# Conditioning dots of layer 1 dealt to two projections, and two weight blocks converted ahead of the silu of the conditioning vectors

## The chip, the cores and the metric

The kernel runs as one program on 1 core of a Trainium2 chip. Its engines are TensorE (matrix products, PE in the rows), VectorE (DVE), ScalarE (ACT), GpSimd (POOL) and SyncE (SP), which here only issues transfers. Every number is a device time in microseconds (us). The metric is the time of one execution of the whole program, as a median over several runs.

## The reference, cut to what matters

Two layers of a diffusion trunk are computed for 128 context tokens and 512 latent tokens at once, 640 columns in all, with 1024 channels. Each layer has a mixer and a PEER channel mixer, and both are modulated by vectors that depend on the conditioning alone:

```python
mod = (jax.nn.silu(cond) @ adaln_w[i] + adaln_b[i])[:, None, :]
sh1, sc1, g1, sh2, sc2, g2 = jnp.split(mod, 6, axis=-1)
hn = rmsnorm(x, norm_mix[i]) * (1 + sc1) + sh1
if i % 2 == 0:
    m = even_mixer(hn, even_w_in[j], even_conv_w[j], even_w_out[j], grid)
else:
    m, s_f, s_b = ssd_mixer(...)
x = x + g1 * m
hn = rmsnorm(x, norm_ffn[i]) * (1 + sc2) + sh2
x = x + g2 * peer(hn, peer_w_q[i], peer_keys[i], peer_u[i], peer_v[i])
```

`adaln_w[i]` is a matrix of 1024 by 6144, so that `mod` has 48 slices of 128 channels in each layer, and each slice is wanted for two conditioning vectors (`c` and `c_ctx`). Layer 1's `mod` is first used when layer 1 begins; sc1 and sh1 are the first 16 of the 48 slices.

## The kernel before, in words

The program is a row of stages, and each stage is a block that all engines enter and leave together. For layer 0 the stages around the change are: `first_adaln` (16 slices of layer 0's modulation on TensorE), a norm, the projection `even_in` (16 weight blocks), the Fourier and convolution stage, `split_into`, the projection `even_out` (8 weight blocks), a norm, the projection `q0` (16 weight blocks), and then the rest of `peer`. In layer 1 the projection `q1` has the shape of `q0`.

**`project_split` (L404)** is the helper behind all four projections. It takes one weight block of 128 by 1024 at a time from `ring`, eight slots that SyncE refills by halves of four blocks (2 MB each). ScalarE copies a block to the upper part of `wide` in fp32r (L465), GpSimd subtracts that from the block for the lower part (L472), and TensorE makes 48 products of the block (L400: 8 chunks, three products of parts, two halves of the tokens). `wide` has two slots, so that ScalarE converts block n+2 when TensorE has finished block n. VectorE takes a finished block out of PSUM: two copies in `even_in`, `q0` and `q1` (L523), three `scalar_tensor_tensor` that add to `xT` in `even_out` (L535). There are two sets of PSUM banks, so TensorE waits for the eviction of block n before it begins block n+2.

**The side work** rides in a projection where `side=(layer, lo, hi)` is given: `even_in` has 32 slices of layer 0 (two for each block), `q0` has all 48 slices of layer 1 (three for each block). A slice is computed on VectorE as two dots along the row, one for each conditioning vector: L502 multiplies a row tile of 128x1024 by a row of `crow` and sums. SyncE loads the conditioning rows `crow` (1 MB, L442), then the slices in pairs of 1 MB, of which two are in the chip at once (L438); a pair's load waits for the dots on the pair that it overwrites. ScalarE makes `crow` into its silu (L460). VectorE does the dots of a block's share, then that block's eviction, in the order of the program:

```python
for o in range(n_blocks):
    for e in range(o * per, (o + 1) * per):
        ...
    dve.wait_ge(wide_used, o + 3)
    evacuate(o, ps[o % 2]).then_inc(pair_free, 1)
```

Before, ScalarE waits for `crow` and makes its silu ahead of the first conversion:

```python
if side is not None:
    act.wait_ge(cond_in, 16)
    nc.scalar.activation(crow[:, :, :], crow[:, :, :], ACT.Silu).then_inc(cond_silu, 1)
with act.Fori(0, n_blocks // SLOTS) as i:
```

After the last block VectorE adds the bias (L509) and forms `scale_mix` or `scale_ffn` (L305).

Of the kernel before, what the change touches and what calls it, by code (L numbers as in the profile page):

```python
# [23 lines left out]
ACT = mybir.ActivationFunctionType  # L24
# [41 lines left out]
SLOTS = 8  # L66
# [73 lines left out]
def hybrid_trunk(nc, stream, keys, wdt, xin, cols_d, rows_d, masks_d, dft_d, state_in, cond_rows, ada_rows, table0, table1, y_out, state_out,  # L140
                 gates_dram, hidden_dram):
    ctx = ExitStack()
    with ctx:
# [252 lines left out]
        def split_matmuls(outs, w_hi, w_lo, moving, c, start, stop):  # L396
# [4 lines left out]
                                            start=start and n == 0, stop=stop and n == 2)  # L401
            return last

        def project_split(tag, n_blocks, moving, evacuate, chunks=NCH, side=None):  # L404


# [3 lines left out]
            with ExitStack() as ph:  # L410
# [5 lines left out]
                if side is not None:  # L416
                    layer, lo, hi = side
                    n_side = hi - lo
                    PAIRS_IN = 2
                    crow = sb(f"crow{tag}", [P, 2, D_MODEL], into=ph)  # L420
                    rows_in = sb(f"ada_in{tag}", [P, PAIRS_IN, 2, D_MODEL], into=ph)
                    junk = sb(f"ada_junk{tag}", [P, 2, D_MODEL], into=ph)
                    cond_in, cond_silu, ada_dotted, ada_biased = (
                        sem(f"{n}_{tag}") for n in ("cond_in", "cond_silu", "ada_dotted", "ada_biased"))
                    pair_in = [sem(f"ada_pair_in{j}_{tag}") for j in range(PAIRS_IN)]
                    per = n_side // n_blocks
                    begin_row = lo - N_FIRST if layer == 0 else N_ADALN - N_FIRST + lo
                with nc.Block() as block:
                    @block.sync
                    def _(sp):  # L430
                        if side is None:
                            feed(sp, first, n_blocks)
                            return

                        def load_pair(p):
                            if p >= PAIRS_IN:
                                sp.wait_ge(ada_dotted, 4 * (p - PAIRS_IN + 1))
                            sp.dma_start(rows_in[:, p % PAIRS_IN, :, :],  # L438
                                         ada_rows[begin_row + 2 * p:begin_row + 2 * p + 2].rearrange("b p n -> p b n"))\
                              .then_inc(pair_in[p % PAIRS_IN], 16)  # L440

                        sp.dma_start(crow[:, :, :], cond_rows).then_inc(cond_in, 16)  # L442
                        pairs = n_side // 2
                        ahead = min(PAIRS_IN, pairs)
                        for p in range(ahead):
                            load_pair(p)
                        for s in range(n_blocks):
                            while ahead < pairs and 2 * (ahead - PAIRS_IN + 1) <= per * (s + 1):
                                load_pair(ahead)
                                ahead += 1  # L450
                            if s % HALF_RING == HALF_RING - 1 and first + SLOTS + s < N_BLOCKS:
                                sp.wait_ge(blocks_used, first + s + 1)
                                load_half(sp, s // HALF_RING % 2, first + SLOTS + s + 1 - HALF_RING)

                    @block.scalar
                    def _(act):
                        act.sem_inc(wide_used, 2)
                        if side is not None:
                            act.wait_ge(cond_in, 16)
                            nc.scalar.activation(crow[:, :, :], crow[:, :, :], ACT.Silu).then_inc(cond_silu, 1)  # L460
                        with act.Fori(0, n_blocks // SLOTS) as i:
                            for s in range(SLOTS):
                                loaded(act, s, i + first // SLOTS)
                                act.wait_ge(wide_used, i * SLOTS + (s + 1))
                                nc.scalar.activation(wide[:, s % 2, 0, :], ring[:, s, :], ACT.Copy).then_inc(hi_done, 1)  # L465

                    @block.gpsimd
                    def _(pool):
# [21 lines left out]
                    @block.vector  # L490
                    def _(dve):
                        dve.sem_inc(pair_free, 2)
                        if side is not None:
                            dve.wait_ge(cond_silu, 1)
                            for o in range(n_blocks):
                                for e in range(o * per, (o + 1) * per):
                                    p, at_ = e // 2, rows_in[:, e // 2 % PAIRS_IN, e % 2, :]
                                    dve.wait_ge(pair_in[p % PAIRS_IN], (p // PAIRS_IN + 1) * 16)
                                    if e >= 2:
                                        dve.wait_ge(ada_dotted, 2 * (e - 1))  # L500
                                    for k, out in ((0, junk[:, e % 2, :]), (1, at_)):
                                        nc.vector.tensor_tensor_reduce(  # L502
                                            out=out, in0=at_, in1=crow[:, k, :], scale=1.0, scalar=0.0, op0=ALU.mult, op1=ALU.add,
                                            accum_out=mods_of[layer][:, lo + e, k:k + 1]).then_inc(ada_dotted, 1)
                                dve.wait_ge(wide_used, o + 3)
                                evacuate(o, ps[o % 2]).then_inc(pair_free, 1)
                            dve.wait_ge(ada_dotted, 2 * n_side)
                            to, bias = adaln_bias(layer, lo, hi)
                            nc.vector.tensor_tensor(to, to, bias, ALU.add).then_inc(ada_biased, 1)  # L509
                            dve.wait_ge(ada_biased, 1)  # L510
                            for comp in (SC1, SC2):
                                if lo <= comp * NCH < hi:
                                    adaln_scale(layer, comp)
                            return
                        with dve.Fori(0, n_blocks // SLOTS) as i:
                            for o in range(per_round):
                                dve.wait_ge(wide_used, i * SLOTS + ((o + 1) * each + 2))
                                evacuate(i * per_round + o, ps[o % 2]).then_inc(pair_free, 1)
# [72 lines left out]
        def even_mixer():  # L591
            with ExitStack() as ph:
# [90 lines left out]
                between.close()  # L683
                y2 = sb("y2_even", [P, NCH, 2, TOK], F32R, into=ph)
                split_into(y2, pT, NCH)
                project_split("even_out", N_EVEN_OUT, [(y2, part) for part in HALVES], add_gated_halves(G1, 0))

        def grid(u):

# [48 lines left out]
        def peer(layer):  # L738
# [7 lines left out]
            with ExitStack() as sparse_life:  # L746
# [5 lines left out]
                with ExitStack() as h_life:  # L752
                    h2 = sb(f"h2{tag}", [P, NCH, 2, DENSE], F32R, into=h_life)
                    idT = sb(f"idT{tag}", [P, 3, DENSE], into=h_life)
                    with ExitStack() as ph:
                        qT = sb(f"qT{tag}", [P, N_WQ, TOK], into=ph)
                        ranges = (slice(0, DENSE), slice(DENSE, TOK))
                        with ExitStack() as s_life:
# [1 line left out]
                            norm_modulate(f"f{layer}", None, scale_of(scale_ffn[layer]), shift_of(SH2, layer),  # L760
                                          split=list(zip((h2, h2s), ranges)), by_token=by_token)
                            project_split(f"q{layer}", N_WQ, [(h2, slice(0, DENSE)), (h2s, slice(0, SPARSE))],
                                          copy_halves(qT, ranges), side=(1, 0, N_ADALN) if layer == 0 else None)
                        keysT = sb(f"keysT{tag}", [P, 2 * PEER_HEADS * KEYS], into=ph)
                        top_keys(layer, tag, ph, h2, qT, keysT, idT, ids, sgate)
                    scatter_gates(layer, tag, h2, idT, by_token, ids, sgate, acc)
# [1334 lines left out]
```

## Time and profile before

| what | value |
|---|---|
| median of 3 runs | 4914.34 us (4910.57 to 4922.31) |
| the profiled execution, its own time | 4908.72 us |
| its span from the first to the last instruction | 4906.9 us |
| TensorE busy | 4500.9 us, 92% of the span |
| TensorE weight loads busy | 3709.5 us, 76% |
| VectorE busy | 3193.5 us, 65% |
| ScalarE busy | 1435.8 us, 29% |
| GpSimd busy | 981.5 us, 20% |
| mean granted TensorE clock | 0.956 |

The profiled execution has a time of its own beside the span of its instructions. The shares are averages over stages with different limits; the stages that the change touches lie in the first 531 us of the span. TensorE's granted clock is given as a share of 2.4 GHz, so that 0.50 is 1.2 GHz.

### The profile page before, as it was taken

What the parts mean: (1) busy time and instruction counts of PE and PEld (TensorE: products, weight loads), DVE (VectorE), ACT (ScalarE), POOL (GpSimd) and SP (SyncE); (2) the same over time, 40 slices, a digit from 0 to 9 for tenths busy, and PEclk for the clock granted to TensorE, in tenths of its full rate; (3) what the DMA queues carried; (4) which work ended last, traced back from release to release, by engine and by line L of the source; (5) the groups of instructions that cost most, each with busy time, mean ns of one, the idle gap of its engine ahead of it and who ended that gap; (6) DMA issues with size and microseconds to landing.
All of it is one profiled execution on the core that took longest, in us unless ns stands there. A gap on an engine that the chain in (4) does not pass through costs nothing. (4 is left out here: it accounts for less than half of the span.)

```text
span 4906.9 us, 60603 instructions
## 1 busy us (share of the span) xinstructions
PE 4500.9 (92%) x21860; PEld 3709.5 (76%) x21860; DVE 3193.5 (65%) x7358; ACT 1435.8 (29%) x2432; POOL 981.5 (20%) x564
## 2 busy tenths in 40 slices
PE   6968899999979999969899779799999997999997
PEld 5857788788868888857777665588878886888886
DVE  4829776699966666635656521226759998666665
ACT  2121233344433333322222220113323443333333
POOL 1113344322210000001211220124442222000000
PEclk8989999999989999989999889899999998999998
DMA  4414433588888888701101010123348888888882
GB/s 185 179 53 179 171 129 129 210 322 331 323 317 299 285 283 297 267 22 41 41 24 43 29 62 34 52 80 135 128 148 309 322 330 323 304 285 297 286 282 104
DMA packets 343772, 937.13 MB, mean 191 GB/s; under 512 B 14544, under 2 KB 145872, under 8 KB 305872
## 3 DMA queue, kind: packets, MB, share of 16 engines
q1 hardware_dynamic: 305360, 662.94, 38.1%
q0 software_dynamic: 38272, 272.65, 14.6%
q8 instruction: 48, 0.79, 0.1%
q14 instruction: 92, 0.75, 0.0%
HBM read 796.59 MB, written 138.94 MB: 191 GB/s over the span
## 5 line engine op out<-in xcount | busy, mean ns | idle before, releaser
L400 PE MATMUL ov_p<-acts_p,wide_v_p 128*128 128x512 f32 x6144 | 1396.8, 390 | 58.8 <-DVE acts_p L1330 58.8
L400 PEld LDWEIGHTS ov_p<-acts_p,wide_v_p 128*128 128x128 f32 x6144 | 1155.7, 188 | 299.5 <-issue 59.1
L400 PE MATMUL hl_p<-h_p,wide_late_p 128*128 128x512 f32 x3072 | 733.1, 394 | 10.9 <-DVE wide_late_p L1152 10.9
L400 PE MATMUL he_p<-h_p,wide_early_p 128*128 128x512 f32 x3072 | 727.1, 397 | 1.9 <-POOL wide_early_p L833 1.7
L400 PEld LDWEIGHTS he_p<-h_p,wide_early_p 128*128 128x128 f32 x3072 | 576.2, 188 | 146.2 <-issue 8.0
L400 PEld LDWEIGHTS hl_p<-h_p,wide_late_p 128*128 128x128 f32 x3072 | 570.0, 189 | 123.8 <-issue 11.4
L1318 DVE TENSOR_TENSOR wide_v_p<-ring,wide_v_p 128x1024 fp32r<-128x1024 f32 x256 | 313.8, 1226 | 445.1 <-ACT wide_v_p L1287 445.1
L1287 ACT ACTIVATE wide_v_p<-ring 128x1024 fp32r<-128x1024 f32 x256 | 271.3, 1060 | 908.6 <-PE ov_p L400 895.6
L833 POOL TENSOR_TENSOR wide_early_p<-ring,wide_early_p 128x1024 fp32r<-128x1024 f32 x128 | 338.5, 2645 | 463.4 <-ACT wide_early_p L889 463.4
L1030 POOL DMA_INDIRECT rows_v_p<-in_table,ids_p x128 | 123.2, 963 | 1218.2 <-DVE acc_p L1351 1172.5
L1030 POOL DMA_INDIRECT rows_late_p<-in_table,ids_p x128 | 225.0, 1758 | 705.6 <-DVE acc_p L1182 642.2
L1161 DVE TENSOR_SCALAR hot_p<-rows,idT_p 128x128 f32<-128x128 f32 x1024 | 347.5, 339 | 0.0
L400 PE MATMUL psq<-h_p,wideq 128*128 128x512 f32 x768 | 268.2, 450 | 44.7 <-POOL wideq L472 30.5
L1112 ACT ACTIVATE wide_late_p<-ring 128x1024 fp32r<-128x1024 f32 x128 | 135.3, 1058 | 546.7 <-PE hl_p L400 542.0
L1591 PE MATMUL gs<-hT,ring 128*128 128x320 f32 x1024 | 287.9, 440 | 5.4 <-ACT su L1679 2.8
L1160 DVE TENSOR_SCALAR hot_p<-rows,idT_p 128x128 f32<-128x128 f32 x1024 | 287.2, 281 | 0.0
L1591 PEld LDWEIGHTS gs<-hT,ring 128*128 128x128 f32 x1024 | 197.8, 195 | 87.4 <-issue 7.6
L1100 PEld LDWEIGHTS pg_p<-hot_p 128*128 128x128 f32 x2048 | 248.2, 191 | 10.0
L1100 PE MATMUL pg_p<-hot_p 128*128 128x128 f32 x2048 | 249.0, 275 | 0.0
L894 ACT ACTIVATE gelu_early_p<-he_p 128x512 f32<-128x512 f32 x128 | 76.6, 598 | 506.3 <-PE he_p L400 506.3
L1326 DVE TENSOR_TENSOR hidden_in_p<-hidden_in_p,gbuf_p 128x512 f32<-128x512 f32 x256 | 175.2, 684 | 54.7 <-DMA hidden_in_p<-hidden 54.7
L400 PEld LDWEIGHTS psq<-h_p,wideq 128*128 128x128 f32 x768 | 146.6, 191 | 79.6 <-POOL wideq L472 31.1
(285 smaller groups left out, 5949.5 us busy)
## 6 DMA issues: line engine op xcount, KB each, us to landing
ring<-in_stream SPq DMA_DIRECT2D x162, 2048.0 KB, 9.0
gates<-staged_p SPq DMA_DIRECT2D x32, 2048.0 KB, 10.6
gbuf_p<-gates SPq DMA_DIRECT2D x64, 1024.0 KB, 13.0
hidden_in_p<-hidden SPq DMA_DIRECT2D x64, 1024.0 KB, 15.5
hidden<-gelu_early_p SPq DMA_DIRECT2D x128, 256.0 KB, 2.0
hidden<-gelu_late_p SPq DMA_DIRECT2D x128, 256.0 KB, 3.8
ada_inq<-in_ada_rows SPq DMA_DIRECT2D x24, 1024.0 KB, 4.9
ada_ineven_in<-in_ada_rows SPq DMA_DIRECT2D x16, 1024.0 KB, 5.0
```

What stands on the lines that cost most here:

```text
L400: last = nc.tensor.matmul(out, lhsT=w, rhs=rhs[:, c, part, cols_], start=start and n == 0, stop=stop and n == 2)
L833: nc.gpsimd.tensor_tensor(wide[:, e % 2, 1, :], ring[:, e, :], wide[:, e % 2, 0, :].bitcast(F32), ALU.subtract).then_inc(blocks_used, 1)
L894: nc.scalar.activation(gelu[:, e % 2, :], hs[e % 2][:, 0:DENSE], ACT.Gelu).then_inc(gelu_done, 1)
L1030: pool.indirect_dma_start(out=rows_in[:, k % slots, :], out_offset=None, in_=(table0, table1)[layer], in_offset=bass.IndirectOffsetOnAxis( ...
L1100: last = nc.tensor.matmul(pg[j][g][:, i * P:(i + 1) * P], lhsT=hot2[:, j, g * EACH + i, :], rhs=hot1[:, j, g * EACH + i, :], start=True, s ...
L1112: nc.scalar.activation(wide[:, m % 2, 0, :], ring[:, m % SLOTS, :], ACT.Copy).then_inc(his_done, 1)
L1160: v.tensor_scalar(hot2[:, m % 2, i, :], row("iota"), idT[:, 1, token:token + 1], None, ALU.is_equal)
L1161: last = v.tensor_scalar(hot1[:, m % 2, i, :], row("iota"), idT[:, 0, token:token + 1], idT[:, 2, token:token + 1], ALU.is_equal, ALU.mult)
L1287: nc.scalar.activation(wide[:, b % 4, 0, :], ring[:, b % SLOTS, :], ACT.Copy).then_inc(whi_done, 1)
L1318: v.tensor_tensor(wide[:, b % 4, 1, :], ring[:, b % SLOTS, :], wide[:, b % 4, 0, :].bitcast(F32), ALU.subtract).then_inc(blocks_used, 1)
L1326: v.tensor_tensor(a, a, gbuf[:, j, :, e, :], ALU.mult).then_inc(mul_done, 1)
L1591: last = mm(ps[h][:, 0:HALF_TOK], lhsT=ring[:, HALF_RING * half + b, c * P:(c + 1) * P], rhs=hT[:, c, HALVES[h]], start=c == 0, stop=c == ...
```

## The change

Layer 1's 48 slices are dealt to two projections: `even_out` gets the first 16 (two for each of its 8 blocks) and `q0` the other 32 (two for each of its 16 blocks instead of three). `even_out` so gets a load of `crow`, eight loads of pairs, a silu, 32 dots, and a bias and a scale at its end. In every projection with side work ScalarE converts blocks 0 and 1 first and makes the silu behind them, ahead of block 2; its loop over blocks is written out there. The semaphores of the side work are now made once and counted on from one projection to the next (`uses`, `dots_before`, `rounds_before`).

```diff
+        PAIRS_IN = 2
+        side_sems = [sem("ada_" + n) for n in ("cond_in", "cond_silu", "dotted", "side_biased")] + \
+                    [sem(f"ada_pair_in{j}") for j in range(PAIRS_IN)]
+        side_done = [0, 0]
...
-                    cond_in, cond_silu, ada_dotted, ada_biased = (
-                        sem(f"{n}_{tag}") for n in ("cond_in", "cond_silu", "ada_dotted", "ada_biased"))
-                    pair_in = [sem(f"ada_pair_in{j}_{tag}") for j in range(PAIRS_IN)]
+                    cond_in, cond_silu, ada_dotted, ada_biased, *pair_in = side_sems
+                    uses, rows_before = side_done
+                    side_done[:] = uses + 1, rows_before + n_side
+                    dots_before, rounds_before = 2 * rows_before, rows_before // (2 * PAIRS_IN)
...
-                                sp.wait_ge(ada_dotted, 4 * (p - PAIRS_IN + 1))
+                                sp.wait_ge(ada_dotted, dots_before + 4 * (p - PAIRS_IN + 1))
...
                         act.sem_inc(wide_used, 2)
-                        if side is not None:
-                            act.wait_ge(cond_in, 16)
-                            nc.scalar.activation(crow[:, :, :], crow[:, :, :], ACT.Silu).then_inc(cond_silu, 1)
-                        with act.Fori(0, n_blocks // SLOTS) as i:
-                            for s in range(SLOTS):
-                                loaded(act, s, i + first // SLOTS)
-                                act.wait_ge(wide_used, i * SLOTS + (s + 1))
-                                nc.scalar.activation(wide[:, s % 2, 0, :], ring[:, s, :], ACT.Copy).then_inc(hi_done, 1)
+
+                        def hi(i, s):
+                            loaded(act, s, i + first // SLOTS)
+                            act.wait_ge(wide_used, i * SLOTS + (s + 1))
+                            nc.scalar.activation(wide[:, s % 2, 0, :], ring[:, s, :], ACT.Copy).then_inc(hi_done, 1)
+
+                        if side is None:
+                            with act.Fori(0, n_blocks // SLOTS) as i:
+                                for s in range(SLOTS):
+                                    hi(i, s)
+                            return
+                        for n in range(n_blocks):
+                            hi(n // SLOTS, n % SLOTS)
+                            if n == 1:
+                                act.wait_ge(cond_in, 16 * (uses + 1))
+                                nc.scalar.activation(crow[:, :, :], crow[:, :, :], ACT.Silu).then_inc(cond_silu, 1)
...
-                project_split("even_out", N_EVEN_OUT, [(y2, part) for part in HALVES], add_gated_halves(G1, 0))
+                project_split("even_out", N_EVEN_OUT, [(y2, part) for part in HALVES], add_gated_halves(G1, 0),
+                              side=(1, 0, N_FIRST))
...
-                                          copy_halves(qT, ranges), side=(1, 0, N_ADALN) if layer == 0 else None)
+                                          copy_halves(qT, ranges), side=(1, N_FIRST, N_ADALN) if layer == 0 else None)
```

How the order of instructions moves is shown at two places. The first is ScalarE at the start of `q0` (`wideq` is what it converts into, `crowq` the conditioning rows). Before:

```order
L455 UNCONDITIONAL_BRANCH [waits barrier_Pool_Activation_PE_DVE_SP_release]
L460 ACT_TABLE_LOAD
L460 ACTIVATE crowq<-crowq 128x2048 [waits cond_in_q0]
L461 UNCONDITIONAL_BRANCH
L461 ISA
L464 ISA [waits half_loaded0]
L465 ACTIVATE wideq<-ring 128x1024 [waits wide_used_q0]
```

Now:

```order
L460 UNCONDITIONAL_BRANCH [waits barrier_Pool_Activation_PE_DVE_SP_release]
L467 ACTIVATE wideq<-ring 128x1024 [waits wide_used_q0,half_loaded0]
L467 ACTIVATE wideq<-ring 128x1024 [waits wide_used_q0]
L478 ACT_TABLE_LOAD
L478 ACTIVATE crowq<-crowq 128x2048 [waits ada_cond_in]
L467 ACTIVATE wideq<-ring 128x1024 [waits wide_used_q0] x2
```

The table load and the silu now stand behind the first two conversions; it is the same in `even_in`, and in `even_out` there is no table load ahead of the silu.

The second place is VectorE in `even_out`, from the start of the stage (`xT` is the residual stream, `pseven_out` the products). Before:

```order
L490 UNCONDITIONAL_BRANCH [waits barrier_Pool_Activation_PE_DVE_SP_release]
L515 UNCONDITIONAL_BRANCH
L535 SCALAR_TENSOR_TENSOR xT<-pseven_out,mods,xT 128x320 [waits wide_used_even_out]
L535 SCALAR_TENSOR_TENSOR xT<-pseven_out,mods,xT 128x192
L535 SCALAR_TENSOR_TENSOR xT<-pseven_out,mods,xT 128x128
```

Now:

```order
L503 UNCONDITIONAL_BRANCH [waits barrier_Pool_Activation_PE_DVE_SP_release]
L515 ISA ada_junkeven_out,mods<-ada_ineven_out,croweven_out 128x1024 [waits ada_pair_in0,ada_cond_silu]
L515 ISA mods 128x1
L515 ISA ada_ineven_out,mods<-ada_ineven_out,croweven_out 128x1024
L515 ISA mods 128x1
L515 ISA ada_junkeven_out,mods<-ada_ineven_out,croweven_out 128x1024 [waits ada_pair_in0]
L515 ISA mods 128x1
L515 ISA ada_ineven_out,mods<-ada_ineven_out,croweven_out 128x1024
L515 ISA mods 128x1
L548 SCALAR_TENSOR_TENSOR xT<-pseven_out,mods,xT 128x320 [waits wide_used_even_out]
L548 SCALAR_TENSOR_TENSOR xT<-pseven_out,mods,xT 128x192
L548 SCALAR_TENSOR_TENSOR xT<-pseven_out,mods,xT 128x128
```

Four dots now stand ahead of each eviction of `even_out`, and the first of them waits for the silu and for the first pair of slices. In `q0` two of each block's six dots are gone.

## Rows read from the trace of the kernel before

**Rows 1.** Busy time by stage: even_in, even_out, q0, q1, from the operation before to the last eviction.

```profile
core 0: us, PE busy (x) PEld busy (x) DVE busy (x) ACT busy (x) POOL busy (x), PEclk, DMA share, GB/s
76.95:204.20 127.25, 114.98 (x768) 114.72 (x768) 114.53 (x162) 19.96 (x18) 41.01 (x16) 0.94 0.56 207
263.36:326.53 63.17, 57.89 (x384) 57.65 (x384) 9.07 (x25) 8.38 (x8) 19.06 (x8) 0.94 0.19 67
360.59:530.16 169.57, 136.08 (x768) 117.53 (x768) 156.38 (x225) 19.91 (x18) 42.91 (x16) 0.93 0.57 205
3139.39:3277.35 137.96, 132.80 (x768) 116.48 (x768) 14.21 (x33) 16.88 (x16) 38.14 (x16) 0.97 0.17 61
```

**Rows 2.** Waits in q0, 384 to 529 us: total, times, longest.

```profile
PE psq L400 <- DVE qT_p L523: 14.2, 10, 1.5
```

**Rows 3.** Timeline, one late block of q0, GpSimd and VectorE: start, duration, engine, line.

```profile
484.39 0.87 DVE L523 COPY qT_p<-psq 128x512 f32<-128x512 f32 x2
485.14 2.37 POOL L472 TENSOR_TENSOR wideq<-ring,wideq 128x1024 fp32r<-128x1024 f32 x1 [7.49 <-ACT wideq L465]
485.20 3.40 DVE L502 CUSTOM_DVE_ANT_0 ada_junkq<-ada_inq,crowq 128x1024 f32<-128x1024 f32 x1
...
488.53 1.21 DVE L502 CUSTOM_DVE_ANT_0 ada_inq<-ada_inq,crowq 128x1024 f32<-128x1024 f32 x1
...
494.25 0.88 DVE L523 COPY qT_p<-psq 128x512 f32<-128x512 f32 x2
```

**Rows 4.** Timeline, VectorE at the end of q0.

```profile
529.28 0.88 DVE L523 COPY qT_p<-psq 128x512 f32<-128x512 f32 x2
...
530.45 0.17 DVE L305 SCALAR_TENSOR_TENSOR scale_ffn<-mods,cols 128x16 f32<-128x16 f32 x1
```

**Rows 5.** Timeline, the start of q0: ScalarE, VectorE, TensorE.

```profile
366.94 1.91 ACT L460 ACTIVATE crowq<-crowq 128x2048 f32<-128x2048 f32 x1 [4.74 <-DMA crowq<-in_cond_rows]
...
369.61 1.23 DVE L502 CUSTOM_DVE_ANT_0 ada_junkq<-ada_inq,crowq 128x1024 f32<-128x1024 f32 x1 [9.03 <-DMA ada_inq<-in_ada_rows]
...
373.09 0.79 PE L400 MATMUL psq<-h_p,wideq 128*128 128x512 f32 x1 [19.45 <-POOL wideq L472]
```

**Rows 6.** Timeline, q1: the first product, and the last two evictions.

```profile
3143.51 0.79 PE L400 MATMUL psq<-h_p,wideq 128*128 128x512 f32 x1 [11.07 <-POOL wideq L472]
...
3268.30 0.89 DVE L523 COPY qT_p<-psq 128x512 f32 x2 [7.27 <-PE psq L400]
3276.46 0.89 DVE L523 COPY qT_p<-psq 128x512 f32 x2 [7.27 <-PE psq L400]
```

**Rows 7.** Timeline, even_in: its start, and one later block on VectorE and GpSimd.

```profile
84.82 1.23 DVE L502 CUSTOM_DVE_ANT_0 ada_junkeven_in<-ada_ineven_in,croweven_in 128x1024 f32<-128x1024 f32 x1 [7.86 <-DMA ada_ineven_in<-in_ada_rows]
...
88.29 22.00 PE L400 MATMUL pseven_in<-h_even,wideeven_in 128*128 128x320 f32 x134 [32.61 <-POOL wideeven_in L472]
...
97.71 0.89 DVE L523 COPY pT<-pseven_in 128x320 f32<-128x320 f32 x2 [3.91 <-PE pseven_in L400]
...
162.03 0.88 DVE L523 COPY pT<-pseven_in 128x320 f32<-128x320 f32 x2
163.23 2.47 DVE L502 CUSTOM_DVE_ANT_0 ada_junkeven_in<-ada_ineven_in,croweven_in 128x1024 f32<-128x1024 f32 x1 [0.32 <-DMA ada_ineven_in<-in_ada_rows]
...
162.21 2.41 POOL L472 TENSOR_TENSOR wideeven_in<-ring,wideeven_in 128x1024 fp32r<-128x1024 f32 x1 [4.63 <-ACT wideeven_in L465]
```

**Rows 8.** Timeline, even_out: the first two evictions and GpSimd's subtraction between them.

```profile
276.11 1.13 DVE L535 SCALAR_TENSOR_TENSOR xT<-pseven_out,mods,xT 128x320 f32<-128x320 f32 x3 [12.74 <-PE pseven_out L400]
277.25 2.39 POOL L472 TENSOR_TENSOR wideeven_out<-ring,wideeven_out 128x1024 fp32r<-128x1024 f32 x1 [7.59 <-ACT wideeven_out L465]
...
283.15 1.13 DVE L535 SCALAR_TENSOR_TENSOR xT<-pseven_out,mods,xT 128x320 f32<-128x320 f32 x3 [5.91 <-PE pseven_out L400]
```

**Rows 9.** Transfers of even_in, 77 to 206 us: issues, KB each, median us to landing.

```profile
ada_ineven_in<-in_ada_rows SPq DMA_DIRECT2D x16, 1024.0 KB, 5.0
ring<-in_stream SPq DMA_DIRECT2D x4, 2048.0 KB, 9.7
```

More of the change, by code:

```diff
@@ L418, in project_split @@
                     n_side = hi - lo
-                    PAIRS_IN = 2
                     crow = sb(f"crow{tag}", [P, 2, D_MODEL], into=ph)
@@ L493, in _ @@
                         if side is not None:
-                            dve.wait_ge(cond_silu, 1)
+                            dve.wait_ge(cond_silu, uses + 1)
                             for o in range(n_blocks):
@@ L497, in _ @@
                                     p, at_ = e // 2, rows_in[:, e // 2 % PAIRS_IN, e % 2, :]
-                                    dve.wait_ge(pair_in[p % PAIRS_IN], (p // PAIRS_IN + 1) * 16)
+                                    dve.wait_ge(pair_in[p % PAIRS_IN], (rounds_before + p // PAIRS_IN + 1) * 16)
                                     if e >= 2:
-                                        dve.wait_ge(ada_dotted, 2 * (e - 1))
+                                        dve.wait_ge(ada_dotted, dots_before + 2 * (e - 1))
                                     for k, out in ((0, junk[:, e % 2, :]), (1, at_)):
@@ L506, in _ @@
                                 evacuate(o, ps[o % 2]).then_inc(pair_free, 1)
-                            dve.wait_ge(ada_dotted, 2 * n_side)
+                            dve.wait_ge(ada_dotted, dots_before + 2 * n_side)
                             to, bias = adaln_bias(layer, lo, hi)
                             nc.vector.tensor_tensor(to, to, bias, ALU.add).then_inc(ada_biased, 1)
-                            dve.wait_ge(ada_biased, 1)
+                            dve.wait_ge(ada_biased, uses + 1)
                             for comp in (SC1, SC2):
```

## The prediction

> **What bounds the kernel now.** TensorE is busy for 92% of the span, so I don't ask which engine is busiest but which stages make TensorE wait for something that the change touches. I read the stretches by stage first, then the waits, then the timeline of single blocks.
>
> The stretches [rows 1] give the plainest comparison. `q0` and `q1` have the same 16 blocks and 768 products; `q0` takes 169.57 us from the last operation of the norm to the end of its last eviction, `q1` takes 137.96. The difference is VectorE: 156.38 us busy in `q0`, 14.21 in `q1`. The waits [rows 2] say the same from TensorE's side: ten times it waited for an eviction. The timeline [rows 3] shows a block of `q0` on VectorE: an eviction at 484.39, then six dots, the next eviction at 494.25, a period of 9.86 us. Five dots from 488.53 to 494.25 are 1.144 us each, the eviction takes 0.81 (484.39 to 485.20), and the dot that begins at 485.20, while GpSimd subtracts (485.14, for 2.37), is held: its successor starts 3.33 later, so 2.19 are lost. TensorE alone needs 8.16 for a block (3268.30 to 3276.46) [rows 6]. So `q0` is bound by VectorE.
>
> `even_in` is bound by TensorE: 7.04 us a block, as in `even_out` (276.11 to 283.15) [rows 8], though VectorE is busy for 114.53 of 127.25 [rows 1]. Its four dots, 4.58, the eviction, 0.80, and a held part of about 1.66 fill a period exactly. It is in step with GpSimd: the dots end at 162.03, just ahead of the subtraction at 162.21 [rows 7], which then runs beside the eviction and holds only the rest.
>
> Both begin late. From the last operation before the stage to TensorE's first product is 373.09 - 360.59 = 12.50 in `q0` and 88.29 - 76.95 = 11.34 in `even_in` [rows 1, 5, 7], because ScalarE waits for the conditioning rows and makes their silu (1.91) ahead of its first conversion [rows 5]. In `q1`, with no silu, it is 3143.51 - 3139.39 = 4.12 [rows 1, 6].
>
> **The change, part by part.**
>
> *Two conversions ahead of the silu, `even_in`.* The start falls from 11.34 to 4.12: 7.2 us gained. Dots still begin at 84.82, 7.87 after the stage's start, since the first pair of slices lands then [rows 7]; four of them, 4.58, end at 12.45. TensorE's block 0 took 97.71 - 88.29 = 9.42 [rows 7], so it would end at 4.12 + 9.42 = 13.54. VectorE is ready 1.1 before it is wanted, where before it had 3.9 to spare. The silu is over long before ScalarE converts block 2, at 13.54. So the whole stage shifts.
>
> *`q0`, start and period together.* Four dots, 4.58, an eviction, 0.80, and at most one whole subtraction, 2.4, make 7.8 us a block, under TensorE's 8.16. `q0` becomes `q1`: 169.57 - 137.96 = 31.6 gained, of which 8.4 is the start (12.50 - 4.12) and the rest the period and VectorE's lag at the end. Dots begin 369.61 - 360.59 = 9.02 after the start [rows 5] and end at 13.6, ahead of block 0. The bias and scale behind the last eviction stay (530.62 - 530.16 = 0.46) [rows 4].
>
> *`even_out`, the price.* It gets 32 dots, four a block: 4.58 + 1.13 = 5.71 of 7.04 us, before any holding. Here VectorE has a longer eviction than in `even_in`, three operations. In step, as in `even_in`: the subtraction starts 1.14 after a block's end (276.11 to 277.25) [rows 8] and ends at 3.5, the dots 4.5 later, at 8.0, so the eviction comes about 1.0 late each time and no later. TensorE's banks allow a block's time of lateness, so it doesn't wait. The last two blocks have no subtraction beside them, and 5.71 against 7.04 makes the lag good. What stays is the bias and scale at the end: 0.5 us lost, by the 0.46 of `q0`. The silu in between costs nothing: it lies on ScalarE while that waits for block 0. Unknown is whether the subtraction holds the `scalar_tensor_tensor` too; no row has the two together [rows 8]. Lower bound nothing, as for the copies, whose 0.88 is the same beside a subtraction as without [rows 7, 4]; upper bound as a dot is held [rows 3], which by the sum under the first rival costs 6 us. I take nothing, since the operation reads PSUM for one input as the copies do.
> The Trainium skill, "SBUF — State Buffer", section on the two separate sides, says that VectorE takes the port pair it shares with GpSimd when it runs a two-port mode or has two SBUF inputs, and then one fully blocks the other. The held dots agree (3.40 against 1.21 us), and the rule speaks against putting dots beside subtractions. By it the eviction, with one SBUF input, isn't held and the sum stands at 4876; without it the sum would be 4882.
>
> *Transfers.* `even_out` gets 9 MB more, at the same rate per block as `even_in`. There, a pair (5.0 us to land) and a ring half (9.7) [rows 9] together made VectorE wait 0.32 once [rows 7]. Nothing taken. The written-out loop of ScalarE: nothing, it is idle for most of each block.
>
> **The sum.** 7.2 + 31.6 - 0.5 = 38.3 us. All later stages begin when these end, behind a common barrier, so it all reaches the end. Against the profiled execution, 4908.72, that is 4870.4; that execution lies 5.6 under the median of the runs, 4914.34. Against the median it is **4876 us**. TensorE's first block at 1.2 GHz (granted clock 0.93 to 0.97 over the stages [rows 1]) moves each of three starts by a us or two either way.
>
> **The rivals.**
>
> *Out of step.* If the dots of a block end over 1.14 + 1.14 = 2.3 us after TensorE's block, the subtraction slips in ahead of the fourth dot and holds a dot fully. Then VectorE needs 4.58 + 0.80 + 2.4 = 7.8 a block in `even_in` against 7.04, and 4.58 + 1.13 + 2.4 = 8.1 in `even_out`. The lag grows by 0.75 for 14 blocks, less 3.3 won back in the last two, plus the 2.3: 9.5 us in `even_in`. In `even_out`: 1.07 for 6 blocks, less 2.7, plus 2.3: 6 us. For it: VectorE's room before block 0 in `even_in` shrinks from 3.9 to 1.1 by this very change, and in `even_out` the dots end between 7.87 and 9.02 + 4.58 = 12.5 and 13.6, TensorE's block 0 at 276.11 - 263.36 = 12.75 [rows 1, 8]. Against it: both are still 1.4 to 3.4 us short of the threshold. With `even_out` alone 4882, with both 4891.
>
> *The start isn't won.* If the first conversions wait for something else (the weight blocks, a table), the 7.2 and 8.4 are lost and only the deal counts: 4876 + 15.6 = 4892. Against: `even_out` and `q1` start in 4.1 us with the same ring, and the order has the table load behind the conversions. It is also the case in which half the change doesn't do what it says.
>
> *Slower: transfers block the dots.* SyncE's queue is in order, and dots wait for pairs. If each pair behind a ring half landed after 5.0 + 9.7 = 14.7 us instead of within a period of 7, VectorE would stand for 7.7 at each of the two ring halves of `even_out` and four of `q0`: 46 us, so 4922. It decides against the change from 6.4 us a ring half (38.3 / 6). Against: `even_in` has the same loads in the same order and lost 0.32 us [rows 7].
>
> **How the numbers follow.** The forecast as summed 0.80; out of step 0.12 (mostly `even_out` alone or a held eviction, 4882); start not won 0.04; slower 0.02; other small losses 0.02. The range, 4865 to 4892: below, 4876 less the 5.6 by which the profiled execution lies under its median and the clock's few us; above, both stages out of step or no early start. A difference of 0.2%, 10 us, is about what a measurement of this kernel can tell from none. Every case but the last ones gains over 20 us: faster 0.96, same 0.02, slower 0.02.
>
> **What would show it.** TensorE's first product about 4.1 us after the operation before it in `even_in` and `q0`, and the first dot still at 7.9 to 9; `q0` at 138 us from there to its last eviction, with no wait of TensorE for evictions; eviction to eviction 8.16 in `q0` and 7.04 in `even_out`, one held dot a block; `even_out` half a us longer, at 63.6 with its bias. Wrong would be: evictions in `even_out` or `even_in` drifting by 0.75 to 1.1 a block, evictions there longer than 1.13, dots with DMA waits of several us, or a second block that starts late behind the silu.

## The result and the profile after

The changed kernel takes 4874.52 us in the median of 6 runs (4873.10 to 4878.16), the kernel before 4913.51 us in as many runs beside it. The ratio is 0.9918 with a 95% interval of 0.9906 to 0.9931: 39 us faster. The forecast was 4876.0 with a range of 4865 to 4892. One execution of run 1 below took 14220.87 us where its five others took 4895.66 to 4900.77; it is left out, and run 1's median is that of the five.

| | before | after |
|---|---|---|
| span of the profiled execution | 4906.9 us | 4873.8 us |
| `even_in`, from the operation before it to its last eviction | 127.25 us | 120.55 us |
| `even_out`, the same | 63.17 us | 64.06 us |
| `q0`, the same | 169.57 us | 137.54 us |
| VectorE's last eviction of `q0` ends at | 530.16 us | 490.24 us |

The stretches of the three stages after, in the columns of [rows 1], and behind them all that follows `q0`:

```profile
77.43:197.98 120.55, 115.69 (x768) 115.42 (x768) 110.53 (x161) 20.07 (x18) 39.19 (x16) 0.96 0.60 218
255.95:320.01 64.06, 58.85 (x384) 58.62 (x384) 54.71 (x90) 10.28 (x9) 20.15 (x8) 0.93 0.58 214
352.70:490.24 137.54, 132.67 (x768) 116.50 (x768) 118.14 (x162) 20.06 (x18) 48.32 (x16) 0.97 0.53 191
490.24:4873.80 4383.56, 4101.50 (x19492) 3359.80 (x19492) 2848.97 (x6838) 1336.69 (x2304) 875.92 (x520) 0.96 0.54 195
```

`q0` is now as long as `q1` was before, 137.54 against 137.96, though VectorE still does 118.14 us of work in it. TensorE's wait for evictions [rows 2] is gone from the list of waits; what is left there between 366 and 490 us has VectorE waiting for TensorE:

```profile
ACT wideq L467 <- PE psq L400: 98.4, 14, 7.2
POOL wideq L485 <- ACT wideq L467: 74.7, 14, 9.2
DVE qT_p L536 <- PE psq L400: 10.5, 16, 2.7
```

The start of `even_in` on ScalarE, then the start of `q0` on ScalarE, to be read against [rows 5]; and below them the start of `even_in` on VectorE, against [rows 7]:

```profile
77.84 2.00 ACT L467 ACTIVATE wideeven_in<-ring 128x1024 fp32r<-128x1024 f32 x2 [6.79 <-ACTq L462]
79.86 1.28 ACT L478 ACT_TABLE_LOAD   x1
82.70 1.91 ACT L478 ACTIVATE croweven_in<-croweven_in 128x2048 f32<-128x2048 f32 x1 [1.55 <-DMA croweven_in<-in_cond_rows]
91.49 1.06 ACT L467 ACTIVATE wideeven_in<-ring 128x1024 fp32r<-128x1024 f32 x1 [6.89 <-PE pseven_in L400]
...
353.11 2.00 ACT L467 ACTIVATE wideq<-ring 128x1024 fp32r<-128x1024 f32 x2 [6.72 <-ACTq L462]
355.13 1.28 ACT L478 ACT_TABLE_LOAD   x1
358.95 1.91 ACT L478 ACTIVATE crowq<-crowq 128x2048 f32<-128x2048 f32 x1 [2.54 <-DMA crowq<-in_cond_rows]
366.95 1.06 ACT L467 ACTIVATE wideq<-ring 128x1024 fp32r<-128x1024 f32 x1 [6.09 <-PE psq L400]
```

```profile
85.39 1.23 DVE L515 CUSTOM_DVE_ANT_0 ada_junkeven_in<-ada_ineven_in,croweven_in 128x1024 f32<-128x1024 f32 x1 [7.96 <-DMA ada_ineven_in<-in_ada_rows]
...
91.49 0.89 DVE L536 COPY pT<-pseven_in 128x320 f32<-128x320 f32 x2 [1.43 <-PE pseven_in L400]
```

The conversions come at once, and the silu lies in the time in which ScalarE would wait for TensorE's block 0. TensorE's first product comes 3.97 us after the operation before it in `even_in` and 3.90 in `q0`, where it was 11.34 and 12.50. The first dot hasn't moved (7.96 us after the start), so that the first eviction waits 1.43 us for TensorE where it waited 3.91 [rows 7]. In all three projections VectorE waits for the first pair of slices and for no later one.

Two blocks of `even_out`, the second one and a middle one, on VectorE and then on GpSimd, to be read against [rows 8]:

```profile
271.78 3.42 DVE L515 CUSTOM_DVE_ANT_0 ada_ineven_out<-ada_ineven_out,croweven_out 128x1024 f32<-128x1024 f32 x1
...
277.43 1.12 DVE L548 SCALAR_TENSOR_TENSOR xT<-pseven_out,mods,xT 128x320 f32<-128x320 f32 x3
...
284.63 1.12 DVE L548 SCALAR_TENSOR_TENSOR xT<-pseven_out,mods,xT 128x320 f32<-128x320 f32 x3
285.68 2.69 DVE L515 CUSTOM_DVE_ANT_0 ada_junkeven_out<-ada_ineven_out,croweven_out 128x1024 f32<-128x1024 f32 x1
...
291.74 1.12 DVE L548 SCALAR_TENSOR_TENSOR xT<-pseven_out,mods,xT 128x320 f32<-128x320 f32 x3
```

```profile
270.73 3.40 POOL L485 TENSOR_TENSOR wideeven_out<-ring,wideeven_out 128x1024 fp32r<-128x1024 f32 x1 [8.56 <-ACT wideeven_out L467]
...
284.87 2.42 POOL L485 TENSOR_TENSOR wideeven_out<-ring,wideeven_out 128x1024 fp32r<-128x1024 f32 x1 [4.69 <-ACT wideeven_out L467]
```

The eviction takes 1.12 us with a subtraction beside it, as 1.13 without [rows 8]: it isn't held. The dot behind it is (2.69 against 1.21), for the rest of the subtraction only. The stage doesn't begin like that. Its first eviction, at 269.59, comes on time, so that the dot behind it starts just ahead of the subtraction: the subtraction is held (3.40 against 2.42), and the next dot is held for the whole of what then remains (3.42). The second eviction so comes 7.84 us after the first. The next three gaps are 7.20, 7.11 and 6.98: some 0.9 us late, VectorE has the subtraction begin beside its eviction, and from there on it keeps TensorE's 7.04. `even_in` begins in the same way, with gaps of 7.60 and 7.44, before the change as after it.

### The profile page after: what moved, and what is told of

It is laid out like the page before. It is cut to its first block and busy times, and to the rows that moved or that the text cites. A ratio compares the mean times of both kernels' runs of the same rounds, so it can differ in the third digit from the quotient of the medians.

```text
span 4873.8 us, 60558 instructions
## 1 busy us (share of the span) xinstructions
PE 4503.8 (92%) x21860; PEld 3715.6 (76%) x21860; DVE 3198.3 (66%) x7359; ACT 1437.5 (29%) x2433; POOL 983.8 (20%) x564
## 5 line engine op out<-in xcount | busy, mean ns | idle before, releaser
L1166 DVE TENSOR_TENSOR wide_late_p<-ring,wide_late_p 128x1024 fp32r<-128x1024 f32 x128 | 156.6, 1225 | 70.7 <-ACT wide_late_p L1126 64.5
```

Source lines behind the costliest of these rows:

```text
L1166: v.tensor_tensor(wide[:, m % 2, 1, :], ring[:, m % SLOTS, :], wide[:, m % 2, 0, :].bitcast(F32), ALU.subtract).then_inc(blocks_used, 1)
```

## The experiments

There are ten runs, two of them of the two kernels again. Times are set against runs of the kernel before on the same chip, whose median moved between 4911.87 and 4916.33 us. The recorded ratios differ from the quotients of the medians by up to 0.0007, which is 3 us. Where a stage's length is named, it runs from the operation before the stage to its last eviction, in the run's profile.

**1. Only the early conversions.** Both projections keep their side work as before the change.

```diff
-                project_split("even_out", N_EVEN_OUT, [(y2, part) for part in HALVES], add_gated_halves(G1, 0),
-                              side=(1, 0, N_FIRST))
+                project_split("even_out", N_EVEN_OUT, [(y2, part) for part in HALVES], add_gated_halves(G1, 0))
...
-                                          copy_halves(qT, ranges), side=(1, N_FIRST, N_ADALN) if layer == 0 else None)
+                                          copy_halves(qT, ranges), side=(1, 0, N_ADALN) if layer == 0 else None)
```

> Only the order on ScalarE is changed (two conversions ahead of the silu); even_out has no side work and q0 has all 48 slices. Theory (q0 is bound by a chain on VectorE that begins when the first pair lands, 9.0 us after the stage's start, and not by TensorE's start): even_in gains 7 us as in the change; in q0 the first product comes 4.1 us after the start instead of 12.5, but the last eviction ends at about 9.0 + 96 x 1.144 + 16 x 0.81 + 14 x 2.19 = 162.5 us after the start instead of 169.6, a gain of 7.1; evictions there 9.8 us apart for most blocks. Sum 14 us: 4899. Rival A (starts simply add): q0 gains 8.4, 4898, and the two can't be told by the time but by q0's 9.8 us period and its length. Rival B (the early start of q0 is lost wholly, since the dots' start has not moved): 7 us in all, 4906.

Measured: 4897.91 us, ratio 0.9966 (0.9952 to 0.9980). In `q0`:

```profile
356.61:518.11 161.50, 135.18 (x768) 116.47 (x768) 152.23 (x226) 20.02 (x18) 41.99 (x16) 0.96 0.59 215
```

```profile
PE psq L400 <- DVE qT_p L536: 15.5, 11, 1.5
```

161.50 us, where the sum along VectorE said 162.5; the first product came 3.99 us after the start, and most evictions follow each other after 9.8 us. Neither the time nor this length tells the theory from its rival A, which makes it 161.2 (169.6 less 8.4), and both keep the period of 9.8. Two other rows do. The first dot comes 8.98 us after the start, as before (9.02), and what the stage gains, VectorE had lost ahead of its first eviction. And against the second profile of the kernel before (run 3), where the first product came 10.79 us after the start and `q0` took 166.70, the first product is 6.8 us earlier and the stage only 5.2 shorter: starts don't simply add. In a stage bound by VectorE the early start of TensorE was worth what it cleared on VectorE's own path: the first subtractions end at 362.8, ahead of the first dot at 365.59, so that the first dots take 1.22 us each where two of them took 3.35 and 3.38 before, and TensorE's block 0 is done when its six dots are (before, VectorE waited 3.7 us for it). These are 4.3 and 3.7 us of the 8.1 by which the stage is shorter than in the first profile.

**2. Only the deal.** ScalarE makes the silu ahead of its first conversion in all three projections.

```diff
                         for n in range(n_blocks):
-                            hi(n // SLOTS, n % SLOTS)
-                            if n == 1:
+                            if n == 0:
                                 act.wait_ge(cond_in, 16 * (uses + 1))
                                 nc.scalar.activation(crow[:, :, :], crow[:, :, :], ACT.Silu).then_inc(cond_silu, 1)
+                            hi(n // SLOTS, n % SLOTS)
```

> Only the deal: 16 slices in even_out, 32 in q0, but in each of the three projections ScalarE makes the silu ahead of its first conversion. Theory: q0's first product stays 12.5 us after the start and q0 gains 169.6 - (12.5 + 132.8 + 1.0) = 23.3 us; even_in gains nothing; even_out now pays for the silu ahead of its conversions, the first product 10.6 us after the start instead of 4.1 (6.5 lost) and 0.5 for bias and scale. Sum 16.3 us: 4897. With e1 that makes 30 of the 39 us of the change: the rest is that the early conversions make the deal cheap. Rival (the parts are independent, the silu in even_out is hidden): 22.8 us, 4891.

Measured: 4898.29 us, ratio 0.9970 (0.9959 to 0.9981). `even_out` and `q0`:

```profile
262.23:333.25 71.02, 58.44 (x384) 58.20 (x384) 58.99 (x90) 10.17 (x9) 21.85 (x8) 0.89 0.52 193
367.63:512.56 144.93, 133.21 (x768) 116.80 (x768) 121.89 (x161) 19.96 (x18) 49.30 (x16) 0.94 0.50 181
```

`even_out` takes 71.02 instead of 64.06 us, since its conversions now wait for a silu that they had no need of; `q0` takes 144.93. The parts are not independent. By the stages' lengths against the first profile of before, the early conversions alone gain 7.1 (`even_in`) and 8.1 (`q0`), the deal alone 24.6 (`q0`) and loses 7.9 (`even_out`), 31.9 in all, and the change 37.8; the difference is `even_out`, which the early conversions make nearly free. The times don't decide it: 18.4 and 18.0 us alone against 39.0 together, a difference within what their intervals allow.

**3 and 4. Both kernels again.** Nothing is edited.

> The kernel before, once more, for a second profile. If the later stages' lengths vary by themselves, its Fourier stage, its norm ahead of q0 and its expert stages of both layers differ by a us or more from those of the first profile; if not, they agree to some tenths of a us, and the 5.6 us that the change's profile loses behind layer 0 are the change's doing.

> The changed kernel, once more, for a second profile. The stages up to the end of q0 take the same as in the first (even_in's first product 4 us after its start, q0 137.5 us from its start to its last eviction). If the loss of 5.6 us between the end of q0 and the end of the program is of single executions, it will be another here.

Measured: 4910.66 and 4870.30 us, one run each. The stretches of `q0` and of all that follows it, of the kernel before, and then of the changed one:

```profile
360.01:526.71 166.70, 134.95 (x768) 116.65 (x768) 155.98 (x225) 19.91 (x18) 42.09 (x16) 0.94 0.58 208
...
526.71:4908.80 4382.09, 4101.27 (x19492) 3359.49 (x19492) 2848.02 (x6839) 1336.28 (x2304) 876.48 (x520) 0.96 0.54 195
```

```profile
350.93:488.37 137.44, 132.56 (x768) 116.27 (x768) 118.15 (x162) 20.07 (x18) 48.33 (x16) 0.97 0.53 191
...
488.37:4868.70 4380.33, 4095.04 (x19492) 3352.76 (x19492) 2848.85 (x6838) 1336.80 (x2304) 876.54 (x520) 0.96 0.54 195
```

The first two profiles differed by 6.8 us in what follows `q0` (4376.74 before, 4383.56 after), which looked like a loss behind the change. Here it is 4382.09 before and 4380.33 after. Two executions of the same kernel differ by 5.4 and by 3.2 us there, as much as the kernels do, so that no loss behind the change is shown. With two profiles of each kernel, a loss of a few us isn't excluded. The changed `q0` agrees to 0.1 us between its two profiles, while before it was 166.70 and 169.57; 1.7 us of that lies ahead of the first product (10.79 and 12.50 us after the start).

**5. Dots out of step.** In `even_out` the first dot also waits for TensorE's block 0.

```diff
                             dve.wait_ge(cond_silu, uses + 1)
+                            if tag == "even_out":
+                                dve.wait_ge(wide_used, 3)
```

> The changed kernel, but in even_out the first dot also waits for TensorE's block 0, so that the dots start some 4.6 us out of step. Theory (VectorE and GpSimd lock each other out whole instructions at a time, and beyond 2.3 us of lag a dot is held for a whole subtraction): the evictions of even_out come 8.1 us apart for the blocks with a subtraction and 5.7 for the last two, and the last one ends some 8 us after TensorE's end instead of 1.2, or TensorE waits for an eviction; even_out about 6 to 8 us longer. Rival (VectorE needs only 5.7 and a part hold of 1.3, so the lag heals by itself): evictions under 7.04 apart until the lag is gone, even_out as long as in the change within 1 us.

Measured: 4886.75 us, one run. `even_out`:

```profile
255.97:328.44 72.47, 60.82 (x384) 59.01 (x384) 58.32 (x89) 10.27 (x9) 21.13 (x8) 0.92 0.50 189
```

```profile
276.91 1.12 DVE L550 SCALAR_TENSOR_TENSOR xT<-pseven_out,mods,xT 128x320 f32<-128x320 f32 x3
277.96 1.21 DVE L517 CUSTOM_DVE_ANT_0 ada_junkeven_out<-ada_ineven_out,croweven_out 128x1024 f32<-128x1024 f32 x1
...
279.10 3.42 DVE L517 CUSTOM_DVE_ANT_0 ada_ineven_out<-ada_ineven_out,croweven_out 128x1024 f32<-128x1024 f32 x1
...
284.74 1.12 DVE L550 SCALAR_TENSOR_TENSOR xT<-pseven_out,mods,xT 128x320 f32<-128x320 f32 x3
```

The stage is 8.4 us longer (72.47 against 64.06) with the same work. The first eviction comes 6.8 us behind TensorE's block 0 (270.12 to 276.91), the next five gaps are 7.83 us, and the last two 5.63; the lag does not heal while subtractions go on. The second dot of each of those blocks is held for 2.2 us (3.42 against 1.21), where in step only 1.4 us of one are lost (2.62). Without the holds the gaps would be 5.6 (4.58 + 1.05), an estimate from the same rows, and the lag would be gone after five blocks. The forecast's 8.1 for this period was too high by 0.3: it took the subtraction's whole 2.4 as the hold, where [rows 3] had 2.19, and 1.13 for the eviction, from start to start 1.05. The time of this one execution is 11 and 16 us over the two profiled ones of the change; of that the stage is 8.4, and the norm behind it 2.2 against the change's first profile (34.9 us between the two stages against 32.7).

**6. A heavy `even_out`.** 32 slices there (four a block), 16 in `q0` (one a block).

```diff
-                              side=(1, 0, N_FIRST))
+                              side=(1, 0, 2 * N_FIRST))
...
-                                          copy_halves(qT, ranges), side=(1, N_FIRST, N_ADALN) if layer == 0 else None)
+                                          copy_halves(qT, ranges), side=(1, 2 * N_FIRST, N_ADALN) if layer == 0 else None)
```

> 32 slices in even_out (four a block) and 16 in q0 (one a block). Theory: even_out becomes bound by VectorE as q0 was: its last eviction ends at about 7.9 + 64 x 1.144 + 8 x 1.05 + 6 x 2.2 = 102.7 us after the stage's start instead of 64.1, 38.6 us lost, while q0, bound by TensorE already, gains nothing (137.5). Time 4913, all of the gain gone. Rival (VectorE's idle time in q0, not the deal's evenness, is what counts): q0 gets shorter than q1's 138, and the time lies below 4905.

Measured: 4919.63 us, ratio 1.0017 (1.0007 to 1.0026), a little slower than the kernel before. `even_out` and `q0`:

```profile
256.23:359.15 102.92, 66.28 (x384) 64.56 (x384) 93.48 (x154) 10.26 (x9) 21.09 (x8) 0.82 0.58 215
393.66:531.26 137.60, 132.73 (x768) 116.44 (x768) 81.49 (x98) 20.07 (x18) 48.34 (x16) 0.97 0.34 130
```

`even_out` takes 102.92 us, where the sum said 102.7, and `q0` is not shorter with half the dots: 137.60. The close agreement is luck in part: VectorE is held for 11.7 us in all and not for 13.2, and waits 1.5 us for a pair that the sum didn't have. Dots are free up to a block's room beside TensorE and cost their whole length beyond it. The time is 6.6 us over the expected one. The profiled execution took 4916.78, 2.9 less than the median; of the 3.8 us that it lies over the forecast, 1.8 are in the norm behind `even_out` (34.5 us between the two stages, 32.7 in the change).

**7. Conditioning rows in PSUM, kernel before.** The silu is written to PSUM, in four pieces of 512 columns, and the dots read it there.

```diff
+                    crow_ps = ph.enter_context(nc.psum_tensor(f"crow_ps{tag}", [P, 2, D_MODEL], F32))
...
-                            nc.scalar.activation(crow[:, :, :], crow[:, :, :], ACT.Silu).then_inc(cond_silu, 1)
+                            for k in range(2):
+                                for h in range(2):
+                                    at_h = slice(512 * h, 512 * h + 512)
+                                    last = nc.scalar.activation(crow_ps[:, k, at_h], crow[:, k, at_h], ACT.Silu)
+                            last.then_inc(cond_silu, 1)
...
-                                            out=out, in0=at_, in1=crow[:, k, :], scale=1.0, scalar=0.0, op0=ALU.mult, op1=ALU.add,
+                                            out=out, in0=at_, in1=crow_ps[:, k, :], scale=1.0, scalar=0.0, op0=ALU.mult, op1=ALU.add,
```

> The kernel before (no deal, silu first), but the silu of the conditioning rows is written to PSUM, and each dot reads it there, so that a dot has one input in SBUF and one in PSUM. Theory (a dot is held because it has two inputs in SBUF beside GpSimd's subtraction): no dot over 1.4 us, q0's six dots and eviction take 6 x 1.15 + 0.8 = 7.7 us, under TensorE's 8.16, and q0 takes 12.5 + 132.8 + 1 = 146 us instead of 169.6: about 4891. Rival A (any dot is held beside a subtraction): dots of 3.4 us remain and the time is 4913 within 3. Rival B (a dot that reads PSUM is slower by some 0.1 to 0.3 us of its own): 16 x 6 x 0.2 = 19 us more VectorE work, q0 stays bound by it, 4900 to 4905.

Measured: 4888.91 us, ratio 0.9954 (0.9937 to 0.9970), with no deal and no early conversion; `q0` takes 147.90 us, where 146 had been expected, and VectorE waits 6.6 us there for three pairs after the first. A block of `q0` on VectorE, and GpSimd's subtraction in it:

```profile
456.78 0.89 DVE L528 COPY qT_p<-psq 128x512 f32<-128x512 f32 x2
457.58 1.21 DVE L507 CUSTOM_DVE_ANT_0 ada_junkq<-ada_inq,crow_psq 128x1024 f32<-128x1024 f32 x1
...
464.43 0.88 DVE L528 COPY qT_p<-psq 128x512 f32<-128x512 f32 x2
```

```profile
456.29 2.39 POOL L477 TENSOR_TENSOR wideq<-ring,wideq 128x1024 fp32r<-128x1024 f32 x1 [5.76 <-ACT wideq L470]
```

No dot in the whole run is longer than 1.22 us; a dot from PSUM costs no more than one from SBUF, and the dot at 457.58 runs beside the subtraction that began at 456.29. Six dots and an eviction take 7.65 us. So the hold was a matter of two inputs in SBUF beside GpSimd's subtraction, and 2.2 us of it a block were what put `q0` over TensorE's 8.16. That is the rule of the Trainium skill ("SBUF — State Buffer", two separate sides), which has VectorE contend with GpSimd when it has two SBUF inputs and GpSimd reads SBUF.

**8. The same with the early conversions.** No deal: the edit of run 7 on the kernel of run 1.

> As the run before, with the two conversions ahead of the silu, and still no deal. Theory: q0 as long as in the change (138 us), even_in too, and even_out without its 0.5 us of bias: 4874, the change's time by another way. Rival (if dots from PSUM are slower, or still held): q0 bound by VectorE, 4885 or more.

Measured: 4879.86 us, ratio 0.9928 (0.9911 to 0.9944); `q0` 139.82 us. Both miss the forecast, 4874 and 138, and the time lies under the rival's 4885. VectorE waited for pairs, 16.6 us in four waits, of which 9.0 is the first pair's; that these waits are what `q0` lacks to the change's 137.5 is what run 10 tries.

```profile
DVE ada_junkq L520 <- DMA ada_inq<-in_ada_rows: 16.6, 4, 9.0
```

**9. The change with rows in PSUM.** The edit of run 7 on the changed kernel.

> The changed kernel with the silu of the conditioning rows in PSUM, so that no dot is held. Theory (in the change VectorE is off the path in all three projections): the held 2.2 us of each of some 34 blocks go, VectorE stands idle for that much more, and the time is the change's, 4874 within 4. Rival (held dots still cost TensorE something, by GpSimd's subtractions of 3.1 us that wait for a dot): the time falls by more than 5 us.

Measured: 4875.66 us, ratio 0.9924 (0.9910 to 0.9938), which is the change's time.

```profile
352.72:490.18 137.46, 132.59 (x768) 116.28 (x768) 87.30 (x162) 20.31 (x21) 38.21 (x16) 0.97 0.53 191
```

VectorE's work in `q0` fell from 118.14 to 87.30 us and the stage by 0.08; `even_in` takes 120.19 us (120.55 and 120.03 in the change's two profiles) and `even_out` 63.96 (64.06 and 63.93). In the change the held dots cost nothing that these rows can show.

**10. Rows in PSUM, three pairs.** As run 8, with three pairs of slices in the chip. The conditioning rows land in `junk`, to have the room, and the side work has its own semaphores in each projection, as before the change.

```diff
-                    PAIRS_IN = 2
-                    crow = sb(f"crow{tag}", [P, 2, D_MODEL], into=ph)
+                    PAIRS_IN = 3
...
                     junk = sb(f"ada_junk{tag}", [P, 2, D_MODEL], into=ph)
+                    crow = junk
```

> No deal, two conversions ahead of the silu, conditioning rows in PSUM, and three pairs of slices in the chip at once instead of two (the conditioning rows are loaded into the tile that later takes the dots' products, to have the room). Theory (q0's periods of 9.7 to 10.6 us in the run with two pairs are waits for a pair that is queued behind a ring half): with one pair more no dot waits for a transfer except the first, q0 takes 137.5 to 138 us instead of 139.8, the time is 4873. Rival (the transfers' rate is the limit): the waits stay, 4876 or more.

Measured: 4877.20 us, ratio 0.9923 (0.9909 to 0.9937). `q0` takes 137.86 us, and VectorE waits for a pair only once, for the first (9.0 us). The theory of the waits holds, though the time is 4 us over its 4873 and would by itself fit the rival. By the time, this kernel, run 9 and the change can't be told apart: all three bring `q0` to TensorE's pace, and none of these kernels is clearly better than the change.

## Why the prediction was right

- **`q0` becomes `q1`, 31.6 us.** Shown: 169.57 to 137.54, 32.0 us, with evictions 8.16 us apart throughout. The new length is firm, the old one isn't: the second pair of profiles has 166.70 to 137.44, 29.3 us, and the forecast had only the longer `q0` to go by. Runs 1 and 2 show that both parts are needed, 161.50 and 144.93 us alone.
- **`even_in` starts earlier, 7.2 us.** The first product is 7.4 us earlier (11.34 to 3.97), the stage 6.7 shorter. The rest is TensorE's block 0, which took 10.1 us (81.40 to 91.49) instead of 9.42, at a mean granted clock of 0.69 in it instead of 0.75. That was in the few us that the prediction left to the clock.
- **`even_out`, the price, 0.5 us.** Bias and scale take 0.3 us there. The stage itself was 0.9 longer in the two first profiles, but five later profiles without side work in it (runs 1, 3, 7, 8, 10) have 63.97 to 64.47 us, and those with it (runs 4 and 9) 63.93 and 63.96, so the 0.9 isn't the change's. Its eviction is not held, which the trace of before had left open; the lower bound of that term was the right one.
- **In step.** VectorE kept step with GpSimd in `even_in` and `even_out`, but the picture of the prediction leaves out how each stage gets there: at the first eviction VectorE isn't 1.0 us late but on time, one dot loses 2.2 us, and the lag of some 0.9 us comes from that. Run 5 shows that the rival was real: out of step, `even_out` takes 8.4 us longer. Its price had been put at 6 with a period of 8.1; in run 5 the first eviction was 6.8 us late rather than 2.3, and the period 7.83. Where between 1 and 6.8 us of lag the one turns into the other was not tried, so that the prediction's threshold of 2.3 stays an estimate.
- **The start, had it not been won.** That rival was priced at 4892. Run 2, where the silu is made first, has 4898: there the silu also delays `even_out`, by 7.9 us, for which the rival had no term.
- **Transfers.** They made nobody wait in `even_out` beyond the first pair. Runs 7 and 8 show how near that limit is: with three slices a block and nothing held, three pairs come late in `q0`, and with a third pair in the chip (run 10) none does.
- **The sum.** 38.3 us forecast against the median, 39.0 measured, with an interval of 34 to 46 us: that they agree to 0.7 is luck in part. The three stages alone give 37.8 in the first pair of profiles and 36.8 in the second. At the last eviction of `q0` the two first profiles stand 39.9 us apart and the two later ones 38.3, the two mixed pairs between 36.5 and 41.8; the stages in between vary by 1 to 3 us on their own, and all that follows `q0` took between 4376.7 and 4385.2 us in twelve profiles, whichever kernel ran. Why those stages vary was not tried.

## What to carry to other kernels

Compare a stage with a twin that lacks the suspected work: `q1` gave `q0`'s new length to 0.4 us. Here side work beside a bound engine was free until it filled that engine's period and cost its full length beyond it, so deal it by each stage's room, and set what it needs (here the silu) behind the first work that the bound engine waits for. Where VectorE and GpSimd work side by side, count the operations with two inputs in SBUF, see at which point of the period the other engine comes in, and think of PSUM as a home for one of the operands.

## What the runs showed of the hardware

- A dot of VectorE with one input in PSUM and one in SBUF was never held by a subtraction of GpSimd (longest 1.22 us of 160 in run 7). With both in SBUF it is (3.4 us), and the subtraction is held by a dot that began first (3.40 against 2.42). Alone, a dot takes the same 1.21 us from either place.
- `scalar_tensor_tensor` with one input in PSUM and one in SBUF was not held: 1.12 us for the three beside a subtraction, 1.13 without.
- The same instructions made a stage of 64.06 and one of 72.47 us (run 5), by where in the period GpSimd's subtraction met VectorE's dots: two engines that hold each other can settle in step, with 1.4 us lost a block, or out of it, with 2.2. In run 5 one late start chose; how late it has to be was not tried.
